# Down weights of the next expert asked for by ScalarE, behind its copy of the step's result, in place of SyncE

## What is computed

```
logits = x @ router_w + router_b            # [256, 32], top 4 a token, softmax over the 4
for each expert e, for its chosen tokens:
    gu   = tokens @ expert_w_gu[e] + expert_b_gu[e]        # [*, 1024] @ [1024, 2048]
    gate = min(gate, 7);  up = clip(up, -7, 7)
    h    = gate * sigmoid(1.702 * gate) * (up + 1)
    y    = h @ expert_w_down[e] + expert_b_down[e]         # [*, 1024] @ [1024, 1024]
    moe_out[token] += router_weight * y
```

## Time and profile before

| | us |
|---|---|
| median of 3 runs | 1790.77 (1790.55 to 1791.33) |
| the profiled execution, its own time | 1791.47 |
| span of its trace | 1789.70 |
| part outside the span | 1.77 |
| PE busy in the span | 1743.8 (97%) |
| DVE, ACT, POOL busy | 498.4, 261.0, 26.7 |
| DMA: moved, mean rate | 539.00 MB, 301 GB/s |
| expert loop, from PE's first L1303 to the copy behind the last L1340 | 527.98 to 1455.72 |

### The profile page before, as it was taken

The page is one execution under the profiler, slowest core; times in us unless marked ns, Lnnn a source line. Parts: engine busy times, 40 slices in busy tenths (PEclk is TensorE's granted clock), DMA queues, the critical chain, the costliest instruction groups (busy, mean ns, idle before and its releaser), DMA issues.

```text
span 1789.7 us, 23618 instructions
## 1 busy us (share of the span) xinstructions
PE 1743.8 (97%) x9997; PEld 1003.7 (56%) x9997; DVE 498.4 (28%) x976; ACT 261.0 (15%) x433; POOL 26.7 (1%) x38
## 2 busy tenths in 40 slices
PE   8999999999999999999999999999999989999998
PEld 7687888888753333333333333333333337778885
DVE  2452467534441111111111111112011140006603
ACT  0322114000111111110101010101010121002200
POOL 1000000110000000000000000000000000000000
PEclk9999999999999999999999999999999999999999
DMA  8473223362669999999999999999999985332341
GB/s 310 172 282 132 108 114 144 98 222 102 224 270 426 428 432 434 427 429 431 436 426 431 430 435 429 429 433 430 428 430 433 431 350 205 148 141 95 134 150 40
DMA packets 51184, 539.00 MB, mean 301 GB/s; under 512 B 4006, under 2 KB 12500, under 8 KB 29360
## 3 DMA queue, kind: packets, MB, share of 16 engines
q1 hardware_dynamic: 45840, 528.09, 71.2%
q10 hardware_dynamic: 3472, 4.85, 1.0%
q0 software_dynamic: 1808, 5.11, 0.9%
HBM read 532.26 MB, written 5.77 MB: 301 GB/s over the span
## 4 chain that ended last, share of the span: by engine, by line
PE 86%; DMA 10%; DVE 2%; ACT 1%; issue 1%; SPq 0%; DVEq 0%; ACTq 0%
PE small L1303 22%; PE proj L695 10%; DMA arena<-in_expert_w_gu 10%; PE small L1340 10%; PE proj L1382 6%; PE proj L899 5%; PE proj L1470 4%; PE proj L1280 3%; PE small L1254 3%; PE small L1290 2%; PE small L978 2%; PE small L716 2%; PE small L1532 2%; PE proj L705 2%; PE small L1400 2%; PE small L1168 2%
## 5 line engine op out<-in xcount | busy, mean ns | idle before, releaser
L1303 PE MATMUL small<-arena 128*64 128x512 f32 x2048 | 449.3, 595 | 12.9 <-DMA arena<-in_expert_w_gu 10.4
L1303 PEld LDWEIGHTS small<-arena 128*64 128x64 f32 x2048 | 149.2, 137 | 297.6 <-issue 276.5
L1340 PE MATMUL small<-arena 128*64 128x512 f32 x1024 | 226.8, 595 | 8.7 <-ACT arena L1732 8.3
L695 PE MATMUL proj<-arena 128*128 128x256 f32 x832 | 186.5, 385 | 0.0
L2378 DVE TENSOR_SCALAR arena<-small 128x512 f32<-128x512 f32 x32 | 22.1, 692 | 546.5 <-PE small L1310 546.5
L695 PEld LDWEIGHTS proj<-arena 128*128 128x128 f32 x832 | 159.4, 193 | 25.3 <-issue 3.0
L1340 PEld LDWEIGHTS small<-arena 128*64 128x64 f32 x1024 | 73.8, 137 | 139.6 <-issue 139.6
L1553 ACT ACTIVATE arena<-proj 128x512 f32<-128x512 f32 x95 | 55.8, 596 | 525.8 <-PE proj L695 149.7
L1382 PE MATMUL proj<-arena 128*128 128x256 f32 x512 | 111.1, 379 | 0.0
L1382 PEld LDWEIGHTS proj<-arena 128*128 128x128 f32 x512 | 97.2, 190 | 13.7 <-issue 0.5
L1728 ACT ACTIVATE arena<-arena 128x512 f32<-128x512 f32 x32 | 20.2, 630 | 498.5 <-DVE arena L2378 498.5
(11 more groups left out here) (443 smaller groups left out, 1559.2 us busy)
## 6 DMA issues: line engine op xcount, KB each, us to landing
arena<-in_expert_w_gu SPq DMA_DIRECT2D x60, 4096.0 KB, 18.8
arena<-in_expert_w_down SPq DMA_DIRECT2D x64, 2048.0 KB, 15.5
arena<-in_w_in_first SPq DMA_DIRECT2D x20, 2048.0 KB, 7.5
arena<-in_w_in SPq DMA_DIRECT2D x16, 2048.0 KB, 7.3
arena<-in_expert_w_gu SPq DMA_DIRECT2D x8, 2048.0 KB, 10.3
arena<-in_w_ada SPq DMA_DIRECT2D x6, 2048.0 KB, 9.1
arena<-in_w_branch SPq DMA_DIRECT2D x4, 2048.0 KB, 9.1
arena<-in_w_out SPq DMA_DIRECT2D x4, 2048.0 KB, 7.9
```

The lines of the kernel that those rows point to most:

```text
L695: mm = pe.matmul(ps[:, m * T:m * T + T], w[:, k, (2 * b + m) * P:(2 * b + m + 1) * P], XT[:, k, :], start=k == 0, stop=k == KD - 1)
L1303: mm = pe.matmul(bank[CAP * half:CAP * half + CAP, :], XG[:, k % 4, k // 4, :], w[:, k % 4, n * D + half * W:n * D + half * W + W], start= ...
L1340: mm = pe.matmul(y_bank[CAP * half:CAP * half + CAP, :], HM[:, m, u, :], w[:, m, half * W:half * W + W], start=u == 0 and m == 0, stop=u = ...
```

## The change

SP keeps units 0 and 1 and loses units 2 and 3, from expert 1 on. ACT issues them instead, both together, right behind its copy of the step's result; the wait for `down_used` is gone from the program, and `y_full`, on which the copy waits, covers both. The last step asks for nothing, so ACT's last loop is split into one up to `n_steps - 1` and one for the last step.

```
--- before.py
+++ after.py
@@ -576,18 +576,9 @@
                 for half in range(2):
                     sp.wait_ge(sig("gu_used"), 2 * u + half + 1)
                     expert_rows(1, u, half)
-            sp.wait_ge(sig("down_used"), 1)
-            expert(1, 2)
-            sp.wait_ge(sig("y_full"), 1)
-            expert(1, 3)
             with sp.Fori(2, n_steps) as i:
-                for u in range(4):
-                    if u < 2:
-                        sp.wait_ge(sig("gu_used"), 4 * i + (2 * u - 2))
-                    elif u == 2:
-                        sp.wait_ge(sig("down_used"), i)
-                    else:
-                        sp.wait_ge(sig("y_full"), i)
+                for u in range(2):
+                    sp.wait_ge(sig("gu_used"), 4 * i + (2 * u - 2))
                     expert(i % EXPERTS, u)
...
-            def expert_step(i, embed):
+            def expert_step(i, embed, more=True):
...
                 act.activation(YSB, y_bank[:, :], ACT.Copy).then_inc(sig("y_ready"), 1)
+                if more:
+                    for u in (2, 3):
+                        act.dma_start(expert_room(u), expert_unit((i + 1) % EXPERTS, u)[0]).then_inc(sig(f"expert_in_{u}"), 16)
                 if embed:
...
-            with act.Fori(24, n_steps) as i:
+            with act.Fori(24, n_steps - 1) as i:
                 expert_step(i, False)
+            with act.Fori(n_steps - 1, n_steps) as i:
+                expert_step(i, False, False)
```

## The result

The changed kernel takes 1803.34 us (median of 4 runs, 1799.29 to 1805.64) against 1790.66: 12.7 us more, a ratio of 1.0068 (interval 1.0056 to 1.0080). The prediction said 1796.0 in a range to 1801.5. The direction is right; the size is not. The profiled execution took 1803.23, beside 1791.47 before: 11.8 us more. Its loop, from copy 0 to copy 31 of the step's result, is 12.98 us longer. Ahead of copy 0 it is 0.22 us shorter and behind the loop 1.0, where PE's clock fell for 3.4 us in place of 6.8; runs 3 and 6 have the 6.8 there, runs 1 and 9 the 3.4.

What follows compares the result with a forecast made beforehand. PE and the DMA engines were both taken as full in the expert loop. Five new waits of 3.5 us (17.5) replace 12.3 us of old ones: +5.2, 1796.7 profiled, median 0.70 lower, 1796.0 us; range 1790.6 to 1801.5.

Steps and rivals of the forecast that it cites:

- Turns of one packet: On each DMA engine, two full queues alternate by one packet whatever its size; a down packet then costs 1.83 us.
- Long and short steps nearly in turn: In the expert loop's backlog, steps of about 31 and 27.35 us would alternate.
- Rival (a): Expert loop: transfers are hidden anyway, the same bytes set 29.22 us a step; time stays 1790.8; chance 0.14 with Rival (b).
- (c): Expert loop: gate and up land up to 9.8 us earlier, the 12.3 us of waits go; 1778.5 at best; chance 0.06.
- Rival (b): DMA queues take turns of a whole unit: five waits of 2.5 us, +0.2, 1791.0; chance 0.14 with Rival (a).
- The prediction's own last sign: The prediction is wrong if the loop's end moves by something that the waits don't add up to.
- Waits of the backlogs: Steps 2 to 8 and 28 to 31: five PE waits of 3.5 us for unit 3, 17.5 us.
- Waits for gate and up nearly gone: At L1303 in the expert loop, the 12.3 us of waits for unit 1 would go.
- The wait for unit 3 alone, put at 3.5: Middle of the down product L1340: unit 3 lands at 19.6 us, needed at 17.1; PE waits 3.5 us.
- Being asked for 3.8 us later would cost nothing by itself: Unit 2's request, each loop step: the later issue costs zero, as it is needed only when L1340 starts.
- Rival (d): PE's clock falls at waits of 3.5 us or more: +13.8 (1804.6) to +18.9; chance 0.15 for +10 and above.
- ACT's issues: zero: ACT's two added issues behind the copy, about 0.35 us each, fit idle time such as 1.38 us before L1740: zero.

Runs made afterwards that it cites:

- run 3: The change with each gate and up unit on SP's queue asked for as two halves, so all packets have 16 KB: 1803.23 us.
- run 6: The change with ACT asking for all four units on its one queue from expert 2 on, in order of use: 1793.85 us.
- run 1: Kernel before, with SP asking for both down units behind y_full, as late as ACT does, on its own one queue: 1793.91 us.
- run 9: run 1 with expert 1's unit 2 asked for at its old early place: 1792.41 us.
- run 2: The change with each down unit on ACT's queue asked for as two halves, 8 KB packets in place of 16: 1843.64 us.
- run 10: Kernel before, with only expert 1's unit 2 asked for 3.4 us later, behind y_full, once in the program: 1793.10 us.
- run 11: The change with expert 1's two down units asked for by SP at their old places, ACT asking from expert 2 on: 1799.15 us.
- run 4: The change with ACT's two issues moved behind the sigmoid of the embedding product: 1807.45 us.
- run 12: The change in steps 8 to 22 alone: ACT asks for the down units there, SP for everything else: 1795.05 us.
- run 8: The change with ACT asking for unit 2 behind down_used, ahead of the copy, and for unit 3 behind the copy: 1795.92 us.
- run 7: The change for unit 3 only: ACT asks for it behind the copy, unit 2 stays with SP behind down_used: 1794.26 us.
- run 5: Kernel before, with each down unit asked for as two halves (8 KB packets), all from SP at the old places: 1794.42 us.

## Why the prediction was right or wrong

**Right: that down units come late, and by which mechanism.** Turns of one packet: 75 of 77 strung packets, 73 and 75 in the change, 81 and 91 with halves. Unit 2 lands after 7.7 to 14.4 us, unit 3 after 13.9 to 28.5 (forecast: some 8, and over 20). Long and short steps nearly in turn, 30.8 / 27.3 and 31.1 / 27.3 against 30.9 / 27.35. Steps 8 to 22 stay at 29.48. Rival (a), the time unchanged, falls, and (c), faster, with it. So does, for the time of this kernel, what the Trainium skill says under "DMA: Bandwidth & Descriptors", "Issuing engines are not separate DMA queues": that issuing from more engines only saves issue time; that the second queue adds no bandwidth the trace agrees with (430 GB/s in the earlier trace rows, 423 in the same step now). Rival (b) falls with the packet counts and run 2, and so, for this transfer, does the same page's "Queues, rings and completion order", where a turn is a packet of 9 to 17 descriptors.

**Wrong: the sum.** In the profiled execution the loop is 12.98 us longer, where +5.2 was forecast. The prediction's own last sign came true: the loop's end moves by something that the waits don't add up to. By the terms:

- *Waits of the backlogs: five at 3.5 = 17.5 expected.* The long steps exceed 27.35 by 1.82, 3.44, 5.44, 5.51, 3.90 and 3.75: 23.9 us. Two contain a clock fall of 1.7. Without them six steps lose 20.5, one of them small and five at 3.4 to 3.9. So what a long step loses came out as forecast, and there is one small one more than the five. The first, at copy 2, is that small one and comes at the very start of the backlog, where the kernel before still has 27.35.
- *"Waits for gate and up nearly gone"* was wrong: 8.0 us of 10.4 remain. A long step has both, 0.4 to 2.3 us for unit 1 and 1.0 to 2.2 for unit 3. The wait for unit 3 alone, put at 3.5, was half of that; that the two add up to the forecast is luck.
- *"Being asked for 3.8 us later would cost nothing by itself"* is the step that failed first. It looked at whether PE waits for this unit at once. In run 10 a single late request costs 2.5 us, and all requests late on one queue 3.3 to 3.7 (runs 1 and 6): the DMA engines run empty at copy 0, ahead of a stretch that they limit, and the changed kernel has the same empty window (0.68). Run 11, without it, has 27.35 in the step to copy 2 and its first long step at copy 3; its median is 4.2 us lower than the change's and its profiled loop 1.3.
- *Clock.* The forecast had no falls; rival (d) had them behind waits of 3.5 us or more. In the backlogs two came, behind 2.2 and 2.3 us: +3.4. How long PE stands idle does not settle it: runs 3 and 4 have waits of 3.02 and 2.82 us with no fall behind them.
- *ACT's issues: zero.* +3.06 at copy 23 to 24, by an issue of 2.54 us instead of 0.35 and the clock fall that it brought. The 1.38 us before L1740 were taken for cover "which no one waits for at once"; that is true of 15 of the 16 embedding steps and false of the last. It is not a cost that can be taken out by itself: run 4 takes it out, and the time does not fall.
- Against these stand 1.65 us of a clock fall at copy 26 that only the execution of before had.

5.2 + 3.0 (waits) + 3.4 + 3.06 - 1.65 = 13.0. The range ended at 1801.5 because the late request and the issue stood at exactly zero and so gave it no width. Rival (d), 1804.6, is the nearest of all in time, by six waits as it said, but with two clock falls in the backlogs instead of three and with a term that it didn't have; that it comes so near is luck.

**How the parts stand in the runs:** late request alone +2.5 to +3.7 (runs 1, 6, 10); second queue alone +3.7 (unit 3) and +5.3 (both, unit 2 early); second queue and late without the first +8.5; all +12.7. Late and shared is more than late or shared, 12.7 against 3.7 + 5.3; the long issue and its clock fall at copy 23 to 24, 3.06 us, come only with both, and are in this count the greater part of the difference. All of it arises in or at the edge of the stretches that the transfers limit (run 12). No version here beats the kernel before.

**Open.** Why ACT's second issue takes 2.5 us. It was seen where it follows the first directly and SP's queue moves 32 KB packets, and not in every such step: 0.84 for the pair on one queue (run 6) and, but for one pair of 1.94, with SP's units in halves (run 3), 0.34 each when 3.4 us apart (run 8). In the change it goes with the end of SP's queue: in the 22 steps in which unit 1 first lands 1.1 to 2.8 us behind the pair's start the second issue takes 2.07 to 3.08 us, and in the nine others (3.9 us or more behind, or already landed) 0.34 to 0.36. What the issue waits for was not found. Open too is what widens the landings of one unit; two queues do it, up to 9.7 us.

## What to carry to other kernels

Where the transfers are the limit later on, read every moved request by one question: do the DMA engines run empty for it anywhere before? The DMA share of the window around it answers that. In run 10 the time lost there came back in full, though nobody waited for that transfer, some 55 us later. A second queue takes away the order of use: it shares by packets, so the queue with the smaller packets gets fewer bytes, and the last of 16 engines decides; so the next thing needed should not be on it. (Putting on it what has long to go is the obvious counterpart; no run here tries that.) And an engine's idle time is cover for an issue only in those steps where nothing stands behind it on the path; so look at the last step of a loop by itself.

## What the runs showed of the hardware

- A queue's turn on a DMA engine is one packet, of 16 or 32 KB (75 to 73, and 75 changes of queue in 77 strung packets); with 8 and 32 KB the counts are 91 to 81.
- The 16 engines' parts of one 2 MB transfer land up to 9.7 us apart (1037.56 to 1047.23) with two queues full, and at most 2.5 us apart in the kernel before. A spread of 3 us, once there, stays on a single queue too: in run 9 it comes with the late requests of step 1, and these two units and the next 74 have 2.9 to 3.1.
- A DMA issue on ACT's queue can hold ScalarE for 2.1 to 3.1 us; in run 2, with four issues in a row, for up to 5.7 us together. Issue to first packet is 1.0 us (run 9, 582.61 to 583.61).
- PE's clock fell next to idle times of 1.96 to 3.03 us in 13 places (the change three, run 3 two, run 4 three, run 8 one, run 11 three, run 12 one) and not next to others of 1.98 to 3.02 us in 13 (among them 2.22 at 637.87 in the change, 3.02 twice in run 3, 2.82 in run 4, 2.34 in run 7). It fell too where PE had not been idle, at the eight matmuls of a bias product on 32 rows (1285.1 in the kernel before). Each fall of 3.4 us costs 1.7.
- An expert's 12 MB take 29.37 us with the down weights in 8 KB packets, and 29.22 with 16 KB (run 5).
